# Six edits to the order of work in a two-layer encoder kernel: halves in the start, one addition in the couples, the evacuation of u, two output projections, y's low part last, and a last output half in two parts

## What is computed

```
x = x + pool_mixer(rms_norm(x, pool_norm), w_in, w_group, scale, w_out)      # layer 0
x = x + dilated_attention_mixer(rms_norm(x, att_norm), w_in, q_norm, k_norm, w_out)   # layer 1

def pool_mixer(h, ...):
    u, gate = split(h @ w_in)                    # 2048 and 2048 columns
    diff = centred_window_mean(u, window 2, 4, 8, 16 by group) - u
    return ((diff @ w_group by group) * scale * silu(gate)) @ w_out

def dilated_attention_mixer(h, ...):             # 8 heads of 128, 3 dilations (1, 4, 16)
    q, k, v for each dilation, gate = split(h @ w_in)
    q, k = rotary(rms_norm(q)), rotary(rms_norm(k))
    o_g, lse_g = windowed attention with dilation g
    o = sum over g of softmax over g (lse_g) * o_g
    return (o * silu(gate)) @ w_out
```

## Time and profile before

| | us |
|---|---|
| runs: median (lowest to highest) | 1664.0 (1662.98 to 1664.48) |
| profiled execution | 1664.83 |
| its span | 1663.0 |
| busy: PE, DVE, ACT, POOL | 1650.5, 1139.6, 840.4, 271.0 |

### The profile page before, as it was taken

How to read it: one execution, slowest core, us unless ns; L and a number is a source line. 1 busy time by engine, 2 the same in 40 slices (tenths; PEclk the granted TensorE clock), 3 DMA queues, 4 the chain that set the end, 5 groups by cost and what they waited for, 6 DMA issues and landing times.

```text
span 1663.0 us, 23746 instructions
## 1 busy us (share of the span) xinstructions
PE 1650.5 (99%) x8288; PEld 1402.0 (84%) x8288; DVE 1139.6 (69%) x1896; ACT 840.4 (51%) x1980; POOL 271.0 (16%) x292
## 2 busy tenths in 40 slices
PE   8999999999999999999999999999999999999999
PEld 7888888888888888888888888888888889999887
DVE  6886677787976697686868357875368346666565
ACT  6453333432431463475655245564456257886463
POOL 1000000004312110141423012230014000005440
PEclk9999999999999999999999999999999999999999
DMA  5133333484511424332332415242324656767784
GB/s 180 52 130 124 121 108 102 152 324 157 177 46 56 148 102 150 104 121 83 127 114 89 137 66 171 82 134 96 127 78 153 229 169 227 246 221 237 241 299 159
DMA packets 146134, 242.60 MB, mean 146 GB/s; under 512 B 17249, under 2 KB 55137, under 8 KB 144994
## 3 DMA queue, kind: packets, MB, share of 16 engines
q1 hardware_dynamic: 141122, 223.79, 40.2%
q10 hardware_dynamic: 4896, 17.30, 2.8%
HBM read 161.23 MB, written 79.82 MB: 145 GB/s over the span
## 4 chain that ended last, share of the span: by engine, by line
PE 81%; ACT 1%; DVE 0%; DMA 0%; issue 0%; ACTq 0%; DVEq 0%
PE pair L1215 23%; PE pair L1217 23%; PE pair L1216 23%; PE pair L1567 4%; PE pair L1539 3%; PE pair L1487 3%; PE pair L1547 2%; ACT pp L2695 1%; DMA raw<-in_pool_w_in_dram 0%; PE pair L1236 0%; ACT turn L2746 0%; ACT qT L2688 0%; DVE w L1729 0%; ACT turn L2761 0%; DVE both L2294 0%
## 5 line engine op out<-in xcount | busy, mean ns | idle before, releaser
L1215 PE MATMUL pair<-w,turnh 128*128 128x512 f32 x640 | 249.0, 389 | 0.0
L1216 PE MATMUL pair<-w,turnh 128*128 128x512 f32 x640 | 249.0, 389 | 0.0
L1217 PE MATMUL pair<-w,turnl 128*128 128x512 f32 x640 | 249.0, 389 | 0.0
L1215 PE MATMUL pair<-w,hTh 128*128 128x512 f32 x544 | 214.0, 393 | 0.0
L1217 PE MATMUL pair<-w,hTl 128*128 128x512 f32 x544 | 212.0, 390 | 0.0
L1216 PE MATMUL pair<-w,hTh 128*128 128x512 f32 x544 | 211.7, 389 | 0.0
L2663 ACT ACTIVATE both<-pair 128x512 f32<-128x512 f32 x160 | 94.0, 591 | 176.4 <-PE pair L1217 167.6
L2157 DVE TENSOR_TENSOR both<-pair,both 128x512 f32<-128x512 f32 x120 | 81.5, 687 | 111.8 <-PE pair L1217 111.4
L2674 ACT ACTIVATE dump<-both 128x128 f32<-128x128 f32 x384 | 119.4, 311 | 64.0 <-DVE both L2157 51.5
L1215 PEld LDWEIGHTS pair<-w,turnh 128*128 128x128 f32 x640 | 120.1, 188 | 25.1 <-DVE turnl L1786 0.2
L1217 PEld LDWEIGHTS pair<-w,turnl 128*128 128x128 f32 x640 | 120.1, 188 | 25.0
(11 more groups left out here) (248 smaller groups left out, 3813.1 us busy)
## 6 DMA issues: line engine op xcount, KB each, us to landing
part_spill<-both SPq DMA_DIRECT2D x160, 256.0 KB, 3.7
both<-part_spill SPq DMA_DIRECT2D x22, 1024.0 KB, 7.2
raw_z<-in_att_w_in_dram SPq DMA_DIRECT2D x20, 1024.0 KB, 5.3
raw<-in_pool_w_in_dram SPq DMA_DIRECT2D x32, 512.0 KB, 5.2
raw<-in_att_w_in_dram SPq DMA_DIRECT2D x10, 1024.0 KB, 6.1
raw_u<-in_att_w_in_dram SPq DMA_DIRECT2D x10, 1024.0 KB, 5.7
diff_spill<-ubuf SPq DMA_DIRECT2D x16, 512.0 KB, 2.7
stage<-gate_spill SPq DMA_DIRECT2D x16, 512.0 KB, 5.8
```

The source lines that it names most:

```text
L1215: nc.tensor.matmul(out, lh, rh, start=first, stop=False, skip_group_check=onto)
L1216: nc.tensor.matmul(out, lh, rl, start=False, stop=False, skip_group_check=onto)
L1217: return nc.tensor.matmul(out, ll, rh, start=False, stop=last, skip_group_check=onto)
```

## The change

1. Start: the norm row is spread out of `bufG` and `whole` instead of `bufS` and `bufU`, one signal for each half; blocks 0 and 1 are scaled, turned and split in halves of 512 columns (`scale_half`, `split_half`, `lows_half`), six warm-up matmuls fall away, and the first quarter of c = 0 (`first_quarter`) runs eight matmuls w high by rows high, eight w low by rows high, and eight w high by rows low, instead of eight threes. ACT's square of block 2 stands ahead of its copy of the row to `bufG`.
2. Couples 1 to 12: `add_quarter(n, 2)` stands behind the splits 5 and 6.
3. `take_u(t - 2)` stands at h = 1 for t up to 34 and at h = 2 behind it (both were h = 0).
4. `SPREAD`: the projections of rows 6 and 7 stand at h = 2 of the same steps.
5. `project_out`: the eight matmuls with y high come first and wait for y high alone, then the four with y low, behind the wait for it.
6. The last output half (row 15, columns 512 to 1023) is made in two parts of 256 columns in two banks, with two additions and two stores.

```diff
@@ -569,7 +569,7 @@
 
             return (y_pooled, m + 1) if m in ON_POOL else (y_ready, ON_SCALAR.index(m) + 1)
 
-        SPREAD = {(42, 0): (6, 0), (43, 0): (6, 1), (44, 0): (7, 0), (45, 0): (7, 1)}
+        SPREAD = {(42, 2): (6, 0), (43, 2): (6, 1), (44, 2): (7, 0), (45, 2): (7, 1)}
         SPREAD_ROWS = (6, 7)
 
         def projected(t, h):
...
@@ -902,9 +902,9 @@
                     sp.wait_ge(out_added, 2 * m + 2)
                     sp.dma_start(dst, xb[m % 4]).then_inc(out_sent[m % 4], 16)
                     return
-                for hf in range(2):
-                    sp.wait_ge(out_added, 2 * m + hf + 1)
-                    sp.dma_start(dst[:, hf, :], xb[m % 4][:, hf, :]).then_inc(out_sent[m % 4], 16)
+                for i, (hf, at) in enumerate(((0, slice(0, 512)), (1, slice(0, 256)), (1, slice(256, 512)))):
+                    sp.wait_ge(out_added, 2 * m + i + 1)
+                    sp.dma_start(dst[:, hf, at], xb[m % 4][:, hf, at]).then_inc(out_sent[m % 4], 16)
 
             def load_out_weight(j):
 
...
+            def first_quarter():
+
+                wh, wl = wview(0, False), wview(0, True)
+                quarter = slice(0, 256)
+                out = pair[0][:, quarter]
+                pe.wait_ge(w_hi, 1)
+                for kd in range(KD):
+                    pe.wait_ge(half_then_row_kept if kd < HB else hhi_done, 2)
+                    nc.tensor.matmul(out, wh[:, kd, :], rowsh[:, kd, quarter], start=(kd == 0), stop=False)
+                for kd in range(KD):
+                    pe.wait_ge(*((dve_step, 5) if kd < HB else lo_ready(0)))
+                    nc.tensor.matmul(out, wl[:, kd, :], rowsh[:, kd, quarter], start=False, stop=False)
+                for kd in range(KD):
+                    pe.wait_ge(hlo_half if kd < HB else hlo_done, 2)
+                    nc.tensor.matmul(out, wh[:, kd, :], rowsl[:, kd, quarter], start=False, stop=(kd == KD - 1))
+
...
             pe.wait_ge(dve_step, 2)
             for hf in range(2):
-                last = nc.tensor.matmul(pair[1][:, 512 * hf:512 * hf + 512], bufU[:, 0:P], bufS[:, 512 * hf:512 * hf + 512],
...
+                nc.tensor.matmul(pair[1][:, 512 * hf:512 * hf + 512], whole[:, 0, 0:P], bufG[:, 512 * hf:512 * hf + 512],
+                                 start=True, stop=True).then_inc(row_spread_then_half, 1)
+            for part in range(2):
+                for tb in range(2):
+                    pe.wait_ge(*((dve_step, tb + 3) if part == 0 else (xn_done, tb + 1)))
+                    for kd in range(HB * part, HB * part + HB):
+                        last = nc.tensor.transpose(x_pair(0, tb)[:, kd * P:kd * P + P],
+                                                   (bufU, bufS)[tb][:, kd * P:kd * P + P], ident[:, :])
...
             for q in range(4):
                 quarter = slice(256 * q, 256 * q + 256)
                 for c in range(3):
                     if c == 0 and q == 0:
-                        pe.wait_ge(hlo_done, 1)
-                        pe.wait_ge(hlo_half, 1)
+                        first_quarter()
+                        transpose_x(0, 2)
+                        continue
                     elif c == 0:
                         pe.wait_ge(hlo_done, 2 * q + 2)
...
 
             def project_out(m, hf):
                 if hf == 0:
-                    pe.wait_ge(ylo_done, m + 1)
...
+                if (m, hf) == (NROW - 1, 1):
+                    for part in range(2):
+                        at = slice(256 * part, 256 * part + 256)
+                        for j in range(HALF):
+                            v = 2 * (HALF + j) + 1
+                            last = three(bank(5 + part)[:, at], y_turned(m % 2, False)[:, j, :],
+                                         y_turned(m % 2, True)[:, j, :], out_w(v, False)[:, at], out_w(v, True)[:, at],
+                                         j == 0, j == HALF - 1)
+                        last.then_inc(zo_done, 1)
+                    return
                 for j in range(HALF):
-                    last = three(out_bank(m, hf), y_turned(m % 2, False)[:, j, :], y_turned(m % 2, True)[:, j, :],
-                                 out_w(2 * (m // TB * HALF + j) + hf, False), out_w(2 * (m // TB * HALF + j) + hf, True),
-                                 j == 0, j == HALF - 1)
+                    for lo in (False, True):
+                        nc.tensor.matmul(out_bank(m, hf), y_turned(m % 2, False)[:, j, :],
+                                         out_w(2 * (m // TB * HALF + j) + hf, lo), start=(j == 0 and not lo), stop=False)
+                if hf == 0:
+                    pe.wait_ge(ylo_done, m + 1)
+                for j in range(HALF):
+                    last = nc.tensor.matmul(out_bank(m, hf), y_turned(m % 2, True)[:, j, :],
+                                            out_w(2 * (m // TB * HALF + j) + hf, False), start=False,
+                                            stop=(j == HALF - 1))
                 last.then_inc(zo_done, 1)
 
             for k in range(NA_PROD):
...
+                    at = slice(512 * part, 512 * part + 512)
+                    if part == 0:
+                        dve.wait_ge(rstd_done, tb + 1)
...
+                    dve.wait_ge(w_hi, 1)
+                    return nc.vector.tensor_tensor(lo_view(0)[:, at], raw[:, 0, at], hi_view(0)[:, at].bitcast(F32),
+                                                   ALU.subtract)
...
-                    dve.wait_ge(row_spread_then_half, 1)
-                    scale(0)
-                    scale(1)
-                    split_lo(0)
-                    lows(0)
-                    lows(1)
+                    link(nc.vector.memset(bufG[:, 0:D], 0.0))
+                    link(nc.vector.memset(whole[:, 0, 0:P], 1.0))
+                    scale_half(0, 0).then_inc(dve_step, 1)
+                    scale_half(1, 0).then_inc(dve_step, 1)
+                    split_half(0).then_inc(dve_step, 1)
+                    steps[0] += 3
+                    scale_half(0, 1).then_inc(xn_done, 1)
+                    scale_half(1, 1).then_inc(xn_done, 1)
+                    lows_half(0, 0)
+                    lows_half(1, 0)
+                    split_half(1).then_inc(w_lo, 1)
...
                     split_product(n + 1, 3)
                     split_product(n + 1, 4)
-                    add_quarter(n, 2)
                     split_product(n + 1, 5)
                     split_product(n + 1, 6)
+                    add_quarter(n, 2)
                     first_window(n)
                 else:
                     diff_low(0)
...
                 part = xb[m % 4][:, hf, :]
+                if (m, hf) == (NROW - 1, 1):
+                    for i in range(2):
+                        at = slice(256 * i, 256 * i + 256)
+                        dve.wait_ge(zo_done, 2 * m + 2 + i)
+                        nc.vector.tensor_tensor(part[:, at], bank(5 + i)[:, at], part[:, at],
+                                                ALU.add).then_inc(out_added, 1)
+                    return
                 nc.vector.tensor_tensor(part, out_bank(m, hf), part, ALU.add).then_inc(out_added, 1)
 
...
                     split_hi(0)
-                    highs(0)
-                    highs(1)
+                    for part in range(2):
+                        for tb in range(2):
+                            act.wait_ge(*((xt_done, tb + 1) if part else (row_spread_then_half, tb + 3)))
+                            nc.scalar.activation(rowsh[:, HB * part:HB * part + HB, P * tb:P * tb + P],
+                                                 x_pair(0, tb)[:, 512 * part:512 * part + 512].rearrange(
+                                                     "p (k c) -> p k c", c=P),
+                                                 ACT.Copy).then_inc(hhi_done if part else half_then_row_kept, 1)
+                    square(2)
                     act.wait_ge(xn_done, 2)
                     nc.scalar.activation(bufG[:, :], pair[1][:, :], ACT.Copy).then_inc(half_then_row_kept, 1)
...
                     exp_factors(*FACTORS[t])
-                if h == 0 and 2 <= t <= NSTEP + 1:
+                if h == (1 if t <= merge_step(0) else 2) and 2 <= t <= NSTEP + 1:
                     take_u(t - 2)
                 if h == 3 and queries_at(t, h):
                     take_queries(queries_at(t, h))
```

62 lines of the change are left out of this document (25 added, 37 removed).

## The result

| | us |
|---|---|
| changed kernel, median of 6 runs (lowest to highest) | 1673.49 (1672.06 to 1674.20) |
| kernel before, median of 6 runs beside it | 1664.81 (1662.98 to 1666.11) |
| ratio, 95% interval | 1.0052 [1.0039, 1.0064] |
| profiled execution of the changed kernel, its span | 1672.06, 1670.3 |

The change made the kernel 8.7 us slower (6.5 to 10.7 by the interval); the forecast was +1.4 and the top of its range 1667.9. The two profiled spans differ by 7.3.

A forecast was written before the change was run, and what follows sets the result against it. PE was taken to bound the kernel, busy 1650.5 of 1663.0 us, other work counting only where PE stops. Terms -2.5 - 0.2 - 0.5 + 4.9 + 0 - 0.3 = +1.4 gave 1665.4 against the median; range 1660.0 to 1667.9.

The forecast's parts named there:

- Term 4: Later take_u and spread projections, from t = 41: raw j=7 lands near 1600.2, PE waits without cover, +4.9 us.
- A: At the same burst of loads: the queue catches up at 434 GB/s, landing 1596.6, total -2.2 (1661.8); chance 0.28.
- B: At the same landing of raw j=7: from 1602.1 on, total over +3.3, with 1602.6 giving 1667.8; chance 0.16.
- Term 1: Start: the first product comes 2.5 us earlier, near 12.3, and the shift is kept; -2.5, ends -1.5 and -2.9.
- Rival C: Start: removed warm-ups or later lows cost, gain only -1.5, time 1666.4; counted inside the forecast, no chance of its own.
- Term 2: Couples: the stop at 287.92 goes (-1.1), new stops of 0.4 and 0.5 come; -0.2, ends -1.1 and +1.0.
- Terms 3, 5 and 6: take_u up to t = 34 frees PE's stop at 1500, -0.5; y low last in output products, 0; split tail, -0.3.

The follow-up runs named there:

- x5: Kernel before with the take_u move alone, projections of rows 6 and 7 at h = 0: 1671.09 us against 1664.76, ratio 1.0035.
- x6: Kernel before with the spread projections moved to h = 2 alone: 1667.38 us against 1664.76, ratio 1.0014.
- x8: x3 with w's second low half ahead of the rows' low halves on DVE: 1662.83 us against 1664.40 before, ratio 0.9992.
- x3: Kernel before with the start's part of the change alone: 1665.12 us against 1664.76, ratio 1.0003.
- x7: Kernel before with the last output half in two parts and y low last: 1663.52 us against 1664.40, ratio 0.9997.
- x2: Changed kernel with the spread projections back at h = 0: 1669.51 us against 1664.08 before, ratio 1.0032.
- x1: Changed kernel with the copy of u(39) back at h = 0 of t = 41: 1668.04 us against 1664.76 before, ratio 1.0020.
- x11: Changed kernel with output weights j=7 loaded at t = 42 right behind j=6: 1664.44 us against 1664.40 before, ratio 1.0004.
- x4: Kernel before with the move of add_quarter(n, 2) in the couples alone: 1665.29 us against 1664.40, ratio 1.0007.

## Why the prediction was wrong

**Term 4** (+4.9) had the right mechanism, and its links came out: the u copy (4.7 later forecast, 4.45 measured, on clocks that differ by 0.28), the idle DMA, the landing (5.0 later for 4.5), the lost cover, the stop (7.1 for 6.8). The line "term = landing of raw j=7 minus 1595.3" gives 1600.8 + 0.3 - 1595.3 = +5.8, 0.9 of it for the later landing. From its place (0.28 ahead) the changed kernel goes to 7.7 behind at 1631.07 (1623.37 before), so the term measured +8.0. The step that failed is the sum behind the stop: "PE has 7 heads of 0.56 ... and two projections of 2.77, together 10.8" priced all of that at full speed. The slow stretch cost 1.8 (the head from 1601.76 to 1602.71 0.95 for 0.56, the eight products 3.31 for 1.93), and x5 and x6 show the same; the last 0.4 are small misses (a projection takes 2.86 for 2.77, the copy behind the landing 0.9 for 0.8). A stop of seven microseconds was forecast, and what it does to the clock was not asked. The size at x6 was missed by the same step (+2.6 for -0.5 to +0.8).

Of the rivals, A's rate did not come: from the first load of the burst to the landing the queue moved 338 GB/s both before (1577 to 1596) and after (1581.5 to 1600.8), not 434. The 436 that the prediction cites beside it from the Trainium skill ("DMA: Bandwidth & Descriptors", Anatomy of one DMA) is given there for DMAs issued from GpSimd, while these are SP's. B was right only in that it was slower: its condition, a landing from 1602.1 on, was not met (1601.1 with the 0.3), and its price, 1667.8, was too small.

The Trainium skill ("TensorE: Matmul & The Clock Gate", Why this matters for your kernels) warns of idle gaps of TensorE between bursts of matmuls, after which they run at the low clock. The trace agrees, with a granted clock of 0.50 behind stops of 2.9 to 7.1 us. With the stretch priced as the rows show it, the term would have been 1.8 higher.

**Term 1** (-2.5) failed in its last sentence, "After 20 us nothing waits on the inputs, so the shift is kept". Raw weights of unit 2 landed at 17.9 before and their high part was made at 20.33, so 2.4 us of slack, just the size of the gain: the gain could be kept only if that load came no later. I had followed the waits that were in the trace and not what would be late next. In the change the load was issued no earlier (13.37 for 13.02, since its release stands behind the rows' lows), took 7.4 for 4.9 and landed 2.9 later, and PE waited 2.25. Measured alone: +0.4 (-1.0 to +2.0). Rival C gave the removed warm-ups or the later lows as the cost. No stop of PE for either is there, but the rows' lows stand ahead of the release of this load, and x8, which turns that round, is 1.9 below x3.

**Term 2** (-0.2) rested on one execution's stop of 1.1. The two new stops are as forecast (0.4 each for 0.4 and 0.5), the old one is 0 to 0.5 in eight other profiles: +0.9 for -0.2. The end of +1.0 was inside the text.

**Terms 3, 5 and 6**: the stop at 1500 shrinks from 0.58 to 0.14 by the starts of the products (0.44 gained for 0.5). The tail's last 256 columns and the smaller store give 0.4 between the last whole addition and the end (5.84 before from 1657.16, 5.46 after from 1664.84), for -0.3. y low last was 0 within what x7 can tell. In the tail's last half the 24 products start 0.12 apart (1664.57 to 1667.32), as the sum had it. The spacing that the prediction takes from the Trainium skill ("TensorE: Matmul & The Clock Gate", Back-to-back issue gap) would be 0.109, and the measurement decides.

In sum, against the profiled execution: start +0.46 for -2.5, couples -0.3 (against the long stop of that execution) for -0.2, from there to t = 41 -0.45 for -0.5, term 4 +8.0 for +4.9, tail -0.4 for -0.3: +7.3 for +1.4, and the spans differ by 7.3. Against medians the couples' part is 1.1 worse. Of the 7.3 between the forecast +1.4 and the measured +8.7, term 4 thus has 3.1, the start 2.9 and the couples 1.1. The range was too narrow because its ends were worked out for the landing alone and the start's ends (-1.5 to -2.9) all took a gain for granted.

## What to carry to other kernels

When an order change makes an engine wait, price the stop and then the stretch behind it: here the stops of 2.9 to 7.1 us each came with 3 to 6 us at half speed, 1.3 to 2.7 us in addition. Those of 1.1 and less did not, and of four between 1.7 and 2.3 one did. When a gate in front of a burst of loads is moved, look for the last load of the burst that somebody needs and move that one up; here one entry in a table was worth 8.6 us and turned a loss into nothing. When a chain at the start is shortened, look at every transfer whose slack is less than the gain, and read the size of a single stop from several profiles before counting on its removal.

## What the runs showed of the hardware that was not expected

- Granted clock: 0.50 behind a stop of 2.9 us (SPREAD alone), for the 5 us from 1597 to 1602, and full again after it; 1.00 behind stops of 0.9 to 1.1 us, and behind those of 1.7, 1.8 and 2.3 us in the start of x2, x1 and the changed kernel, but 0.50 behind one of 2.1 us in the start of x11. The products of 128x512 start 0.43 apart at the low level and 0.227 at the high one.
- The same load of 512 KB took 3.9 to 7.4 us to land in the start. With the old start (before, x4 to x7) it took 3.9 to 4.9, and in four profiles with the change's start (the changed kernel, x1, x2, x11) 6.8 to 7.4, where the next x block was issued 0.7 to 0.8 behind it.
- The identity matrix, the first transfer of all, arrived between 3.7 and 4.8 us in different executions, and PE's first work with it.
